# Two transformer blocks on one core: another order of loads, transposes and first products at the beginning

## What is computed

```
def adaln(cond, w, b):
    m = jax.nn.silu(cond) @ w + b
    return jnp.split(m, 3, axis=-1)
...
        shift, scale, gate = adaln(c[:, None, :], ada_w[layer], ada_b[layer])
        shift_c, scale_c, gate_c = adaln(c_ctx, ada_w[layer], ada_b[layer])
        h = rms_norm(x, norm_g[layer]) * (1.0 + scale) + shift
        if layer % 2 == 0:
            y = mixer_ab(h, w_in_ab[i], v_norm_g[i], spatial_w[i], spatial_b[i], w_out_ab[i])
            if need_ctx_out:
                hc = rms_norm(ctx, norm_g[layer]) * (1.0 + scale_c) + shift_c
                yc = mixer_ab(hc, w_in_ab[i], v_norm_g[i], spatial_w[i], spatial_b[i], w_out_ab[i])
```

## Time and profile before

| | |
|---|---|
| median of three runs | 1587.43 us |
| the profiled execution | 1587.3 us |
| its span | 1585.3 us |
| TensorE matmul busy, share of the span | 1529.0 us, 96% |
| TensorE weight loads busy | 1376.7 us, 87% |
| VectorE, GpSimd, ScalarE busy | 1026.2, 884.3, 507.0 us |
| mean granted TensorE clock | 0.997 |
| read from HBM | 127.71 MB |

### The profile page before, as it was taken

How to read it: one execution, slowest core, us unless ns; L and a number is a source line. 1 busy time by engine, 2 the same in 40 slices (tenths; PEclk the granted TensorE clock), 3 DMA queues, 4 the chain that set the end, 5 groups by cost and what they waited for, 6 DMA issues and landing times.

```text
span 1585.3 us, 28865 instructions
## 1 busy us (share of the span) xinstructions
PE 1529.0 (96%) x10718; PEld 1376.7 (87%) x10718; DVE 1026.2 (65%) x1603; ACT 507.0 (32%) x1047; POOL 884.3 (56%) x830
## 2 busy tenths in 40 slices
PE   6999999999999999999999999999999999999998
PEld 4999977998988888998988888888998999999887
DVE  4599957469938876865777887876436666565002
ACT  4411112121137773333336555554214110111001
POOL 1354531567784508664337754434572877777981
PEclk9999999999999999999999999999999999999999
DMA  9447421223210002232121221111231333333431
GB/s 318 134 130 215 147 74 54 93 67 94 80 54 2 19 11 80 81 88 60 40 54 41 54 55 41 53 41 54 68 94 41 93 93 93 93 93 108 131 119 53
DMA packets 188970, 131.11 MB, mean 83 GB/s; under 512 B 5278, under 2 KB 171710, under 8 KB 188750
## 3 DMA queue, kind: packets, MB, share of 16 engines
q1 hardware_dynamic: 188878, 129.82, 27.4%
HBM read 127.71 MB, written 2.10 MB: 82 GB/s over the span
## 4 chain that ended last, share of the span: by engine, by line
PE 87%; DVE 7%; ACT 2%; issue 2%; DMA 1%; SPq 0%; DVEq 0%; ACTq 0%
PE ps L2341 20%; PE ps L2342 19%; PE ps L2343 19%; PE ps L3100 3%; PE ps L3099 3%; PE ps L3098 3%; PE ps L2685 2%; PE ps L2709 2%; DVE sb_sum L2169 2%; PE ps L3013 2%; PE ps L2672 1%; PE ps L2989 1%; PE ps L2663 1%; PE ps L2914 1%; DMA ada_first<-in_ada_w 1%
## 5 line engine op out<-in xcount | busy, mean ns | idle before, releaser
L792 POOL TENSOR_SCALAR w_hi<-raw 128x512 fp32r<-128x512 f32 x322 | 243.7, 757 | 578.6 <-PE ps L2343 224.3
L794 POOL TENSOR_TENSOR w_lo<-raw,w_hi 128x512 fp32r<-128x512 f32 x322 | 462.6, 1437 | 26.9
L2341 PE MATMUL ps<-xn_hi,w_hi 128*128 128x256 f32 (+1 forms) x672 | 212.6, 316 | 6.3 <-ACT ks L1307 2.1
L2341 PE MATMUL ps<-op_hi,w_hi 128*128 128x384 f32 (+1 forms) x608 | 213.3, 351 | 1.6 <-DVE op_lo L1560 1.5
L2343 PE MATMUL ps<-op_hi,w_lo 128*128 128x384 f32 (+1 forms) x608 | 212.0, 349 | 0.0
L2342 PE MATMUL ps<-op_lo,w_hi 128*128 128x384 f32 (+1 forms) x608 | 212.0, 349 | 0.0
L2342 PE MATMUL ps<-xn_lo,w_hi 128*128 128x256 f32 (+1 forms) x672 | 191.5, 285 | 0.0
L2343 PE MATMUL ps<-xn_hi,w_lo 128*128 128x256 f32 (+1 forms) x672 | 190.9, 284 | 0.0
L2341 PE MATMUL ps<-u_hi,w_hi 128*128 128x260 f32 (+2 forms) x528 | 169.1, 320 | 0.9 <-DVE u_lo L2233 0.4
L2342 PE MATMUL ps<-u_lo,w_hi 128*128 128x260 f32 (+2 forms) x528 | 167.4, 317 | 0.0
L2343 PE MATMUL ps<-u_hi,w_lo 128*128 128x260 f32 (+2 forms) x528 | 167.2, 317 | 0.0
(11 more groups left out here) (471 smaller groups left out, 3430.7 us busy)
## 6 DMA issues: line engine op xcount, KB each, us to landing
raw<-in_w_in SPq DMA_DIRECT2D x45, 512.0 KB, 3.8
raw<-in_w_up SPq DMA_DIRECT2D x44, 512.0 KB, 3.8
ada_ring<-in_ada_w SPq DMA_DIRECT2D x14, 1024.0 KB, 5.3
raw<-in_w_down SPq DMA_DIRECT2D x22, 512.0 KB, 3.2
raw<-in_w_in_ab SPq DMA_DIRECT2D x20, 512.0 KB, 6.0
raw<-in_w_in_c SPq DMA_DIRECT2D x20, 512.0 KB, 3.8
ada_first<-in_ada_w SPq DMA_DIRECT2D x4, 2048.0 KB, 16.7
raw<-in_w_out SPq DMA_DIRECT2D x16, 512.0 KB, 3.9
```

The costliest lines, as they stand in the source:

```text
L792: steps(nc.gpsimd.tensor_scalar(hi, r, 1.0, 0.0, ALU.mult, ALU.add))
L794: nc.gpsimd.tensor_tensor(lo, r, hi.bitcast(F32), ALU.subtract)\
L2341: mm(o[:, to:to + n], w_h[:, k, :], hi[:, k0 + k, c0:c0 + n], start=a, stop=False)
```

## The change

It puts the work up to the sums of squares in another order; what is computed stays.

- SP: the identity first, `x` in two halves by width (each 128 partitions with four rows of 2 KB), then the nine small loads, the meta tokens, `ada_first` 0, `raw` 0, `ctx`, `raw` 1, `ada_first` 1 and 2, and `ada_first` 3. The later small loads wait until `ctx` is turned.
- TensorE turns `x` first, then the parameters and the meta tokens. `keep_busy` with 30 stands ahead of `ada_rows(0)`, and 4 instead of 2 behind it. `ctx` is turned behind `turn_rows(0)`.
- The copies of turned `x` alternate between VectorE (even chunks) and ScalarE (odd), those of `ctx` between ScalarE (first two) and VectorE.
- Chunks 0 to 3 of slabs 0 and 1 are multiplied in single segments: first the latents' segment of both slabs, then the second segments.
- The shift columns of slab 1 are no longer part of its segments. `uv_shift(n)` does them for both slabs, eight chunks in a row.
- `ctx_in` and `meta_in` lie in the place of the later `ada_ring`; `xn_hi`, `xn_lo` and the `xs` tiles over them start 32 bytes further; one semaphore is shared.

```diff
@@ SP @@
+            sp.dma_start(ident[:, :], consts[:, 0:P]).then_inc(s["consts_in"], 16)
+            for half, landed in enumerate(("x_in", "x_in_b")):
+                d = slice(half * D // 2, (half + 1) * D // 2)
+                sp.dma_start(x_in[:, :, d], x.rearrange("(t p) d -> p t d", p=P)[:, :, d]).then_inc(s[landed], 16)
...
-                    sp.dma_start(x_in[:, :, :], x.rearrange("(t p) d -> p t d", p=P)).then_inc(s["x_in"], 16)
-                    sp.dma_start(ctx_in[:, :, :], ctx.rearrange("(t p) d -> p t d", p=P)).then_inc(s["ctx_in"], 16)
-                    sp.dma_start(meta_in[:, :], meta_tokens_2).then_inc(s["ctx_in"], 16)
+                    sp.dma_start(meta_in[:, :], meta_tokens_2).then_inc(s["vec_in"], 16)
                     ada_slab(0)
                     first_raw(0)
+                    sp.dma_start(ctx_in[:, :, :], ctx.rearrange("(t p) d -> p t d", p=P)).then_inc(s["ctx_in"], 16)
+                    first_raw(1)
                     ada_slab(1)
                     ada_slab(2)
-                    first_raw(1)
 
                     sp.wait_ge(s["ada_rows"], 1)
                     ada_slab(3)
+                    sp.wait_ge(s["x_turned"], KC + 5)
@@ ScalarE @@
+            for k in range(1, KC, 2):
+                act.wait_ge(s["x_turned"], k + 1)
+                nc.scalar.copy(lat(k), bank(k % 4)[:, :]).then_inc(s["copied_act"], 1)
...
+            take_rows(0)
+            act.wait_ge(s["mod_ready"], 1)
+            for k in range(4):
+                nc.scalar.activation(xm_hi[:, k, 0:S], lat(k), ACT.Identity, scale=modg[:, 0, 0, k:k + 1])\
+                  .then_inc(s["xl_hi"], 1)
+            for g in range(2):
+                act.wait_ge(s["x_turned"], KC + 1 + g + 1)
+                nc.scalar.copy(ctxT[:, 2 * g:2 * g + 2, :].rearrange("p k n -> p (k n)"), ctx_turned(g))\
+                  .then_inc(s["copied_act"], 1)
...
             square(0)
             square(1)
-            take_rows(0)
-            for k in range(4):
-                early_hi(k)
             take_rows(1)
-            for k in range(4, KC):
-                early_hi(k)
+            act.wait_ge(s["x_ready"], KC // 2 + 3)
+            early_hi(4)
+            early_hi(5)
             take_rows(2)
+            early_hi(6)
+            early_hi(7)
@@ TensorE @@
             pe.wait_ge(s["fill_ready"], 3)
+            keep_busy(bank(2), 30)
             ada_rows(0)
-            keep_busy(bank(4), 2)
+            keep_busy(bank(2), 4)
             turn_rows(0)
-            keep_busy(bank(4), 5)
...
+            def uv_segment(n, seg, k):
+
+                c0, cols_, to = SEG_XC[seg]
+                g = SLAB0["uv"] + n
+                o, wh, wl = gemm_ps[(BLOCK0["uv"] + n) % 2][:, to:to + cols_], w_hi[:, g % 2, k, :], w_lo[:, g % 2, k, :]
+                hi, lo = xm_hi[:, k, c0:c0 + cols_], xm_lo[:, k, c0:c0 + cols_]
+                pe.wait_ge(s["xg_hi" if seg else "xl_hi"], k + 1)
+                mm(o, wh, hi, start=(k == 0), stop=False)
+                mm(o, wl, hi, start=False, stop=False)
+                pe.wait_ge(s["xg_lo" if seg else "xl_lo"], k + 1)
+                mm(o, wh, lo, start=False, stop=False)
...
+            def uv_shift(n):
+
+                g = SLAB0["uv"] + n
+                products(xc_rows(gemm_ps[(BLOCK0["uv"] + n) % 2], SX, XM), xm_hi, xm_lo, w_hi[:, g % 2, :, :],
+                         w_lo[:, g % 2, :, :], KC, 0, [(SX, 2, 0)], True, True)
+
+            for n in range(2):
...
+                for k in range(4):
+                    uv_segment(n, 0, k)
+            for k in range(4):
+                uv_segment(0, 1, k)
...
             ada_rows(1)
-            uv_first(1, 2)
+            uv_segment(1, 1, 0)
+            uv_segment(1, 1, 1)
             turn_rows(1)
-            uv_first(2, 4)
+            uv_segment(1, 1, 2)
+            uv_segment(1, 1, 3)
             ada_rows(2)
-            uv_first(4, 6)
+            uv_chunks(0, 4, 5)
             turn_rows(2)
-            uv_first(6, KC)
+            uv_chunks(0, 5, KC)
             ada_rows(3)
...
+            uv_chunks(1, 4, 5)
             turn_rows(3)
...
+            uv_chunks(1, 5, 6)
             pe.wait_ge(s["xg_lo"], KC + 2)
...
+            uv_shift(0)
+            uv_chunks(1, 6, KC)
+            uv_shift(1)
             sums_end("l0")
```

More of the change, by code:

```diff
@@ L272, in two_blocks @@
         assert size([P, Q_EARLY, S]) + 2 * size([P, KC, XG]) <= 2 * size([P, KC, S]) + size([P, 4, SX])
[L274 to L278, removed]
+        XN0 = 8
+        xn_hi, = plan(("xn_hi", [P, KC, ROW], F32R), start=stage0 + 4 * XN0)
+        xn_lo, = plan(("xn_lo", [P, KC, ROW], F32R), start=stage0 + size([P, KC, ROW]) + 4 * XN0)
+        zs, xbc = plan(("zs", [P, KC, T2]), ("xbc", [P, XC + 1, TP]), start=stage0 + 2 * size([P, KC, ROW]))
+        assert XN0 + T2 <= ROW
+        xs_hi, = plan(("xs_hi", [P, KC, ROW], F32R), start=stage0 + 4 * (U0 + XN0))
+        xs_lo, = plan(("xs_lo", [P, KC, ROW], F32R), start=stage0 + size([P, KC, ROW]) + 4 * (U0 + XN0))
         xp_lo, = plan(("xp_lo", [P, KC, T2], F32R), start=layer0 + size([P, TP]))
@@ L1569, in _ @@
             nc.vector.memset(cond_w[:, :, :], 0.0).then_inc(s["cond_ready"], 1)
-            take_cols(0, bank(0))
+            for k in range(0, KC, 2):
+                dve.wait_ge(s["x_turned"], k + 1)
+                nc.vector.tensor_copy(lat(k), bank(k % 4)[:, :]).then_inc(s["x_ready"], 1)
+            take_cols(0, bank(5))
             dve.wait_ge(s["consts_in"], 16)
@@ L1621, in _ @@
             for k in range(4):
-                early_lo(k)
+                dve.wait_ge(s["xl_hi"], k + 1)
+                nc.vector.scalar_tensor_tensor(xm_lo[:, k, 0:S], lat(k), modg[:, 0, 0, k:k + 1],
+                                               xm_hi[:, k, 0:S].bitcast(F32), ALU.mult, ALU.subtract)\
+                  .then_inc(s["xl_lo"], 1)
+            for g in range(2, 4):
+                dve.wait_ge(s["x_turned"], KC + 1 + g + 1)
+                nc.vector.tensor_copy(ctxT[:, 2 * g:2 * g + 2, :].rearrange("p k n -> p (k n)"), ctx_turned(g))\
+                  .then_inc(s["x_ready"], 1)
+            for k in range(4):
+                dve.wait_ge(s["xg_hi"], k + 1)
+                nc.vector.scalar_tensor_tensor(xm_lo[:, k, S:SX], ctxT[:, k, :], modg[:, 0, 1, k:k + 1],
+                                               xm_hi[:, k, S:SX].bitcast(F32), ALU.mult, ALU.subtract)\
+                  .then_inc(s["xg_lo"], 1)
             mod_part(1)
@@ L2457, in uv_first @@
-            def uv_first(k0, k1):
-                slab_of("uv", 0, xm_hi, xm_lo, SEG_XC, k0, k1, ready=0, of="xg_lo", mark=False)
-            pe.wait_ge(s_evac[BLOCK0["uv"] % 2], 1 + BLOCK0["uv"] // 2)
-            pe.wait_ge(s["split_half"], SLAB0["uv"] + 1)
-            pe.wait_ge(s["xg_hi"], 1)
-            for w in (w_hi, w_lo):
-                for c0, n, to in SEG_XC:
-                    mm(gemm_ps[0][:, to:to + n], w[:, 0, 0, :], xm_hi[:, 0, c0:c0 + n], start=w is w_hi, stop=False)
-            pe.wait_ge(s["xg_lo"], 1)
@@ L2467, in _ @@
-            for c0, n, to in SEG_XC:
-                mm(gemm_ps[0][:, to:to + n], w_hi[:, 0, 0, :], xm_lo[:, 0, c0:c0 + n], start=False, stop=False)
+            pe.wait_ge(s["ctx_in"], 16)
+            for g in range(4):
+                for a in range(2):
+                    for t in range(CTX // P):
+                        ins = nc.tensor.transpose(ctx_turned(g)[:, a * CTX + t * P:a * CTX + (t + 1) * P],
+                                                  ctx_in[:, t, (2 * g + a) * P:(2 * g + a + 1) * P], ident[:, :])
+                ins.then_inc(s["x_turned"], 1)
```

78 lines of the change are left out of this document (35 added, 43 removed).

## The result

The change made the kernel slower. Six runs of it have a median of 1593.92 us (1591.71 to 1597.74), six of the kernel before on the same chip one of 1588.61 us (1587.33 to 1590.09): a ratio of 1.0037, with a 95% interval of 1.0027 to 1.0047. The forecast was 1589.0, and its range ended at 1591.3. The profiled execution took 1592.8 us with a span of 1591.0, against 1587.3 and 1585.3 before: +5.7 us in the span.

The account below looks back on a forecast made before the run. TensorE was taken as the bound, through when it starts the sums of squares. Start -0.3, stall -0.7, shift columns +2.7 gave +1.7, rounded to +1.6: 1589.0 us, range 1586.0 to 1591.3.

Parts of the forecast that it names:

- The opening: Loads and transposes up to the first slab product: `x` issued 3.33 us earlier, first slab product at 27.1 instead of 27.44.
- it isn't what decides: First `ada_first` slab, landing at 15.4: the 30 matmuls of zeros ahead, ending at 21.2, set when the first modulation product starts.
- The stall: TensorE's 0.56 us stall at 41.91, from VectorE slowed during GpSimd's split of `raw` 1: goes, 0.7 us saved with slower restart.
- What comes: Slab 1's shift columns as 24 two-column matmuls of their own: +2.7 us, the largest term on TensorE's path.
- The clock later on: Attention's small matmuls, stretch 464 to 468: a half-clock stretch may vanish or appear, worth up to 1.7 us.
- The rival of one more half-clock stretch: One more half-clock stretch on the path: +3.3 us in all, 1590.7 us; chance 0.12.
- The rival of the slow opening: TensorE's early transposes stay at the 421 ns pace: total +4.1 us, 1591.5 us; chance 0.12.
- The shifted operands: `xn_hi` and `xn_lo` starting 32 bytes later, under the second block's products, might cost time; no size given, chance 0.02.

Follow-up runs that it names:

- run 3: The change with its 48 two-column shift matmuls spread between wide ones and no zeros ahead of the first modulation product: 1594.99 us, ratio 1.0038.
- Run 5: The change with 12 instead of 30 matmuls of zeros ahead of the first modulation product: 1592.18 us, ratio 1.0023.
- Run 6: The change with the 48 two-column shift matmuls replaced by 24 that hold the two columns as weights: 1587.52 us, ratio 0.9989.
- run 9: The kernel before, opening and order kept, with 24 shift matmuls that hold the two columns as weights: 1590.31 us, ratio 1.0002.
- 10: The change itself, unedited, measured again on the chip of run 9: 1595.42 us, ratio 1.0038.
- 2: The kernel before with slab 1 in 384-column segments and both slabs' shift in two runs of 24 two-column matmuls: 1595.77 us, ratio 1.0037.
- run 8: The change with 42 of the 48 two-column shift matmuls left out, its shift product incomplete: 1588.13 us, ratio 0.9997.
- run 1: The change with its 48 two-column shift matmuls spread in pieces of six, wide ones between most: 1596.91 us, ratio 1.0053.

## Why the prediction was wrong, point by point

- **The opening** was right in its result, and in most of its parts. `x` turned from 6.51 (6.9 forecast) and done by 12.86 (12.6); the zeros are 60 records in 6.94 us (7.3) and end at 20.97 (21.2); the first slab product starts at 26.33 (27.1). The first modulation slab was later than worked out, 16.5 by the wait in run 3 instead of 15.4, but "it isn't what decides" held: it lay ready for more than 4 us behind the filler. Run 5 shows it from the other side.
- **The stall** of 0.56 near 41 is gone, as forecast: the second weights are split early, and VectorE's low parts of the context keep their 0.48 us. GpSimd's first split of `raw` 1, and the last of these low parts on VectorE:

```profile
22.53 0.62 POOL L802 TENSOR_SCALAR w_hi<-raw 128x512 fp32r<-128x512 f32 x1 [0.30 <-DMA raw<-in_w_in_ab]
...
44.05 0.48 DVE L1625 SCALAR_TENSOR_TENSOR xm_lo<-ctxT,modg,xm_hi 128x256 fp32r<-128x256 f32 x1
```

- **A wait that I missed** stands at `turn_rows(3)`: ScalarE copies the modulation's rows behind its squares. It costs 0.42 us, about what the start of the sums without the clock (59.2) lies over the forecast (58.8). The chain that ended last goes through it, and TensorE's timeline has the idle time:

```profile
48.13 0.63 ACT sq L1045
...
49.07 0.48 ACT m_rows L1034
...
49.59 1.05 PE L2442 MATMUL ps<-group,m_rows 128*128 128x2 f32 x8 [0.42 <-ACT m_rows L1034]
```

- **What comes** is the step that failed. It priced the 24 added matmuls at 2.7 us, from six of them between wide ones at full clock, and put their effect on the clock at nothing without a reason. At full clock the price is right: the second run takes 2.76 (59.43 to 62.19), all but its first three at full pace. But the step took the same price for any arrangement. The rows that it came from have six at a time between wide ones. In the change the granted clock goes to 1.2 GHz in the midst of the first run and stays there beyond the wide ones: the first run takes 3.80 us, the twelve wide matmuls behind it 3.98 instead of 2.10, and a second stretch behind the sums costs 3.2 more.
- **The clock later on** had the mechanism next to it and looked in the wrong place. It read from the earlier trace rows that short matmuls with idle time between lower the clock, and drew from it that a stretch in the attention might move, worth 1.7 us either way. The idle time was misplaced: the 0.46 us that 464 to 468 has lie behind the slow stretch, since TensorE is busy for all 4.00 us from 463 to 467; ahead of it stands one gap of 0.57 at 461.9. And the step did not ask what the change's own added small matmuls would do. The trace of before had a nearer case. Ahead of its other half-clock stretch TensorE has no idle time at all, but 18 records of one column in a row (its timeline, then busy time by stage):

```profile
642.04 1.05 PE L2747 MATMUL ps<-ones,sq_y 128*128 128x1 f32 x8
643.03 1.19 PE L2747 MATMUL ps<-ones,sq 128*16 128x1 f32 x10
...
640.00:645.00 5.00, 5.00 (x42) 4.94 (x41) 3.15 (x8) 0.75 (x2) 4.17 (x4) 0.93 0.39 105
645.00:649.00 4.00, 4.00 (x23) 3.83 (x22) 2.47 (x5) 0.17 (x1) 1.30 (x2) 0.67 0.30 74
```

  The rival of one more half-clock stretch, at 0.12, had the right kind and too small a size (+3.3 in all): there were two on the path, each about twice as long as the one measured, and in both executions of the change that were profiled.
- **The rival of the slow opening** did not happen. The tile `x_in` on TensorE in the changed kernel, from 10 and from 12 us:

```profile
L2458 PE MATMUL ps<-ident,x_in x6: 421/421/421, 9.7 to 10.8; 128*128 128x128 f32 x6
...
L2458 PE MATMUL ps<-ident,x_in x8: 272/273/421, 11.7 to 12.6; 128*128 128x128 f32 x8
```

  The duration falls from 421 to 272 ns while TensorE does nothing but transposes, as it did before. The Trainium skill (TensorE: Matmul & The Clock Gate, Part 4: PE-mode transpose) says that the full clock does not engage for transposes; here the measured durations decide against it.
- **The shifted operands** were not tried alone. Run 6 has them and needs 1586.1 - 57.50 = 1528.6 us behind the start of the sums; run 9 has not and needs 1587.0 - 58.61 = 1528.4. So they cost nothing that shows, in one profiled execution of each.

What stays open: what number and mixture of small matmuls lowers the clock. The total of 48 isn't the measure, since the first fall comes when only 7 to 12 (10 and the change) or some 22 (2 and 5) of them have been issued, while the 24 of the kernel before, in sixes between wide ones, don't lower it. How much of the second stretch belongs to the shift columns and how much to the sums' own one-column matmuls isn't separated: it is gone with the swap, but run 8 has one there with six of the columns and a wait. And it is open why the old opening shows a low stretch near 30 us in runs 2 and 9 and not in the profile of before.

## What to carry to other kernels

A matmul of two moving columns against 128 columns of weights takes as long here as one of 256 against two: 0.112 and 0.114 us start to start. That the weight load is what holds up the first is not shown, but fits: the trace lists the loads with 0.19 us for 128 columns and 0.08 for two. So where one operand is that thin make it the weights; this halves their number here and keeps the clock. Before adding many small matmuls to a busy TensorE, count how many stand near each other afterwards, those of other helpers included, and in the profile after read the granted clock of just that stretch: a price taken from a few of them says nothing of the wide ones behind. Filler ahead of a product should last until its data lands and no longer: thirty spent most of what the queue had won, twelve kept some 3 us of it, and with none the clock fell.

## What the runs showed that I had not expected

TensorE's clock falls without idle time: in the run from 51.65 us the engine is listed as busy all along, and the spacing of one and the same instruction goes from 0.11 to 0.21 us at 52.9. The last idle time, 0.42 us, lies more than 3 us ahead of that; run 1 has none there and falls too, run 6 has it and doesn't. With 256 moving columns in the same place, at the same 0.114 us each (run 6), the clock stays at 2.4 GHz. The Trainium skill (TensorE: Matmul & The Clock Gate, Why this matters for your kernels) names idle gaps between bursts of matmuls as what to avoid against a drop in the middle of a kernel. The trace shows a second way, small matmuls without a gap, worth some 5 us or 0.3% here.
